# First and third norm by token halves in a two-block transformer kernel

## The chip, the cores and the metric

The kernel runs on one core of a Trainium2 chip. The metric is the device time in microseconds (us), from the first to the last instruction with what lies around them; the table below gives the median of three runs. TensorE is called PE, VectorE DVE, ScalarE ACT, GpSimd POOL and SyncE SP, as in the profile.

## What is computed

512 tokens of width 1024 pass through two transformer blocks. What matters here is the end of the first block and the start of the second:

```python
h = h + rms_norm(mix @ w_out[l], ln_attn_post[l])      # first norm
hn = rms_norm(h, ln_ffn_pre[l])                        # second norm
u = causal_dwconv(hn @ w_up[l], conv_w[l], conv_b[l])
gate, val = jnp.split(u, 2, axis=-1)
f = (jax.nn.gelu(gate, approximate=True) * val) @ w_down[l]
h = h + rms_norm(f, ln_ffn_post[l])                    # third norm
...
h = rmsnorm(x, norm_mix_g[l])                          # fourth norm, second block
proj = h @ w_in                                        # the stage "mix"
a = a_val * jax.nn.sigmoid(a_gate)
a = causal_dwconv_2(a, conv_a_w) + conv_a_b            # 31 taps
```

`rms_norm` divides by the root of the mean square over the 1024 features of a token, then scales by a gain. (The kernel numbers the input's norm 0, so the four above are r = 1, 2, 3 and 4.)

## The kernel before

Activations lie transposed: 128 features on the partitions, 512 tokens along the free dimension, so 1024 features are eight tiles `[128, 512]`. Weights stream from memory as blocks of 1 MB, each of two output tiles by up to eight input tiles, in a ring of four slots. Every product is made of three matmuls with fp32r operands (`mm3`, L478): upper part by upper part, and the two mixed products. So each weight block is split: ACT copies it to `wh` (`split_hi` L1263, the instruction is L1273), DVE subtracts that from the raw block to get `wl` (`low` L1968, L1976). `ahead(n)` (L1275) on ACT splits block n+3. SP loads a block once the block four before it has left its slot (`load` L381 waits for `acc_ready`). Each engine works through its own list in program order; the order is written out by hand, and semaphores tie the lists together. Nothing is planned at run time.

A block of 8 input tiles is 48 matmuls of 512 columns (8 inputs, 2 outputs, 3 products); the last products of a block of the feed-forward group 2 have 6 input tiles, so 36. Results go to four banks `acc`, of which ACT evacuates each (`take` L1288, instruction L1294, and `taken_out` L1543); a block that wants a bank waits for that evacuation (`begin_block` L488).

A norm after a product (r = 1 and 3) takes these steps. The squares of the last output tiles are made by ACT (L1541, L1307) and added by DVE into `sqa` (`add_squares` L1886). PE sums over features with four tiny products (`norm_sums` L525), ACT takes the root (`norm_root` L1309), DVE the reciprocal (`norm_recip` L1895), PE spreads it over all partitions (`norm_spread` L532), and DVE adds the residual (`residual` L1937: per feature tile a scaled product L1941 and an addition L1943). Between these steps PE runs products with constants whose result is not used (`keep_busy` L484, called in `norm` L540).

The norm after it (r = 2 and 4) is not waited for at first: the first two weight blocks of the next stage are multiplied with the new residual itself, scaled by the gain (`raw_blocks` L547). ACT makes the upper part `XRH` (`raw_upper` L1330), DVE the lower part `XRL` (`raw_low` L1948, L1951), ACT the squares, and PE sums them over features, one matmul of ones per feature tile, within the first block (L562). When all eight are summed, ACT takes the root (L1318), DVE the reciprocal of 128x512 (L1898), and DVE and ACT make the normed operands `XH`, `XL` (`operand` L1907, `operand_upper` L1325), which the third block on reads. The results of the two raw blocks are scaled afterwards (`by_rms` L1955).

The lists around this, in order. ACT (L1550 to L1569): for each out block the split ahead and the evacuations; the root of norm 1; eight times copy and square; `ahead` for block ffn+3; root of norm 2; evacuation of the first two tiles; eight operand copies; then the groups of the feed-forward (`group` L1571), where the gelu of pair 0 (L1589) comes before the split ahead and the evacuation of tiles 2 and 3. DVE (L2325 to L2331, L2416 to L2428): sums of squares, reciprocal, `residual`, the lower part of block ffn+2 and of ffn+3, reciprocal of norm 2, `operand`, group 0 with its convolution (`conv3` L2334). For r = 3 and 4 the lists are alike, with `mix` for `ffn`; after `operand(4)` DVE has the taps of the 31-tap convolution (L2445), the gates and the lower weight parts up to the stage's end.

Of the kernel before, what the change touches and what calls it, by code (L numbers as in the profile page):

```python
# [62 lines left out]
OTHERS = {r: sum(x not in SUMMED for x in range(r + 1)) for r in range(9)}  # L63

NARROW = {r: sum(x not in WIDE for x in range(r + 1)) for r in range(9)}

RAW = {0: 0, 2: KT, 4: 2 * KT, 7: 3 * KT}
# [35 lines left out]
def build(nc, xT, memT, wstream, params, consts, lora, poolw, normf, out):  # L103
    with ExitStack() as ctx:
# [205 lines left out]
        def raw_of(r, k):  # L310

            return (X0H[:, k, :], X0L[k // 4][:, k % 4, :]) if r == 0 else (XRH[:, k, :], XRL[:, k, :])
# [162 lines left out]
        def _(pe):  # L475
# [49 lines left out]
            def norm_sums(r, nt=TT):  # L525

                pe.wait_ge(sq_used, KT * (r + 1))
# [12 lines left out]
            def norm(r):  # L540
                keep_busy(mb[:, 3, :], 4 if r == 1 else 12)
                norm_sums(r)
                keep_busy(mb[:, 3, :], 2)
                norm_spread(r)
                keep_busy(mb[:, 3, :], 12)

            def raw_blocks(name, r):  # L547

                for b in range(2):
                    n, t = B0[name] + b, T0[name] + 2 * b  # L550
                    begin_block(n, t)
                    for k in range(KT):
# [7 lines left out]
                        if b == 0 and r in SUMMED:  # L560
                            pe.wait_ge(sq_ready, KT * r + k + 1)
                            mm(mb[:, 0, :], ones, sq[:, k % 2, :], start=(k == 0),  # L562
                               stop=(k == KT - 1)).then_inc(sq_used, 1)
                        elif b == 0 and k == KT - 1:
                            pe.wait_ge(sq_used, KT * (r + 1))
                            mm(mb[:, 0, :], ones, sqa[:, :], start=True, stop=True).then_inc(st_sum, 1)
# [338 lines left out]
            for b in range(1, 4):  # L905
# [8 lines left out]
            norm(1)  # L914


            def group(name, i, hidden, need=None, spread=None, first=0):
# [13 lines left out]
                for b in range(4):  # L931
# [291 lines left out]
            with pe.If(crowded > 0):  # L1223
# [5 lines left out]
                pe.wait_ge(x_ready, 32 + KT)  # L1229
# [12 lines left out]
        def _(act):  # L1242
# [66 lines left out]
            def norm_root(r, nt=TT, preload=True):  # L1309
# [3 lines left out]
                if r in WIDE:  # L1313
                    if r in SUMMED:
                        act.wait_ge(sq_used, KT * (r + 1))
                    else:
                        act.wait_ge(st_sum, OTHERS[r])
                    actv(sqa[:, :], mb[:, 0, :], ACT.Sqrt, bias=cs("eps", 0, 1), scale=1.0 / D).then_inc(sd_ready, 1)  # L1318
# [4 lines left out]
                actv(sd[:, 0:nt], sums, ACT.Sqrt, bias=cs("eps", 0, 1), scale=1.0 / D).then_inc(sd_ready, 1)  # L1323

# [218 lines left out]
            def taken_out(t, dst):  # L1543
                actv(dst, acc[:, t % 4, :], ACT.Copy).then_inc(evac, 1)
# [5 lines left out]
            for b in range(4):  # L1550
                ahead(B0["out"] + b)
                for m in (2 * b, 2 * b + 1):
                    squared_out(T0["out"] + m, 8 + m)
                    if b < 3:
                        taken_out(T0["out"] + m, Fo[:, m, :])
            for m in (6, 7):
                taken_out(T0["out"] + m, Fo[:, m, :])
            norm_root(1)

            for m in range(KT):  # L1560
                act.wait_ge(x_ready, m + 1)
                raw_upper(2, m, "ln_ffn_pre")
                square(16 + m, XT[:, m, :])
# [4 lines left out]
            for k in range(KT):  # L1568
                operand_upper(2, k)  # L1569

            def group(name, i, hidden):  # L1571
# [4 lines left out]
                for b in range(hidden + 4):  # L1576
# [13 lines left out]
                    if b >= hidden and k == 2 and name == "ffn":  # L1590
                        for m in (2 * (b - hidden), 2 * (b - hidden) + 1):

                            act.wait_ge(s["acc_added"], m + 1)
                            square(24 + m, Fo[:, m, :])
# [4 lines left out]
            norm_root(3)  # L1599

            for m in range(KT):
                act.wait_ge(x_ready, 8 + m + 1)
                raw_upper(4, m, "norm_mix")
                square(32 + m, XT[:, m, :])
# [61 lines left out]
            for k in range(KT):  # L1666
                square(40 + k, MT[:, k, :])
# [6 lines left out]
            for m in range(KT):  # L1674
                act.wait_ge(x_ready, 16 + m + 1)
                square(48 + m, XT[:, m, :])
# [25 lines left out]
            def x_parts(b):  # L1702
                for m in (2 * b, 2 * b + 1):
                    act.wait_ge(x_ready, 24 + m + 1)
                    actv(XRH[:, m, :], XT[:, m, :], ACT.Copy).then_inc(s["rx_hi"], 1)
                    square(56 + m, XT[:, m, :])
# [160 lines left out]
        def _(dve):  # L1867
# [27 lines left out]
            def norm_recip(r, nt=TT):  # L1895
                dve.wait_ge(sd_ready, r + 1)
# [10 lines left out]
            def operand(r, gname):  # L1907

                dve.wait_ge(rb_ready, r + 1)
# [27 lines left out]
            def residual(r, gname, gnext):  # L1937

                dve.wait_ge(rb_ready, r + 1)
                for m in range(KT):  # L1940
                    link(v.scalar_tensor_tensor(out=tmp[:, m % 2, :], in0=Fo[:, m, :], scalar=pr(gname, m),  # L1941
                                                in1=mb[:, 1, :], op0=ALU.mult, op1=ALU.mult))
                    v.tensor_tensor(XT[:, m, :], XT[:, m, :], tmp[:, m % 2, :], ALU.add).then_inc(x_ready, 1)  # L1943
                    if m:
                        raw_low(r + 1, m - 1, gnext)
                raw_low(r + 1, KT - 1, gnext)
# [378 lines left out]
            for m in range(KT):  # L2325
# [3 lines left out]
            norm_recip(1)  # L2329
            dve.wait_ge(in_xb, 32)  # L2330
            residual(1, "ln_attn_post", "ln_ffn_pre")  # L2331
# [18 lines left out]
            def group(name, i, hidden, last=False):  # L2350
# [45 lines left out]
                for m in range(KT):  # L2396
                    if last and name == "ffn" and m >= 2:
                        add_squares(24 + m - 2)
                    dve.wait_ge(evac, add(t0 + 2 * hidden + m + 1, 24))
                    e = ev[:, (e0 + 2 * hidden + m) % 4, 2:S + 2]  # L2400
                    if name == "ffn" and k == 0:
# [10 lines left out]
                if last and name == "ffn":  # L2412
# [603 lines left out]
```

## Time and profile before

| | |
|---|---|
| median of 3 runs | 1656.53 us (1651.3 to 1659.92) |
| profiled execution, its time | 1651.62 us |
| its span, first to last instruction | 1649.7 us |
| PE, DVE, ACT busy | 1528.5, 1095.7, 705.2 us |
| mean granted PE clock | 0.987 of full speed |
| traffic | 181.37 MB, mean 110 GB/s |

PE counts as busy while any matmul is in flight, the filler of `keep_busy` too; the record of a pipelined matmul overlaps the next, so the pace is read from the distance of two starts. A row "[1.10 <-DVE XRL L1951]" says that the engine stood idle for 1.10 us until that instruction released it. The page's chain of work that ended last follows the releases back from the end: what stands in it set the time.

### The profile page before, as it was taken

The numbers are of one execution on the slowest core, as the hardware profiler recorded it, in microseconds if no ns is written. First come the engines' busy times: TensorE is split into PE (matmuls) and PEld (weight loads), VectorE is DVE, ScalarE is ACT, GpSimd is POOL, SyncE is SP. The second block draws the span as 40 slices with busy tenths as digits, with TensorE's granted clock in tenths as the row PEclk, the third lists the DMA queues.
The fourth block names the chain that finished last, engine by engine and source line by source line (L and its number), as shares of the span: only waits on it lengthen the run. The fifth ranks groups of instructions, "written<-read, shape, count | busy, mean of one in ns | idle before, by whom it ended". The sixth has DMA issues, their size and how long they took to land.

```text
span 1649.7 us, 26802 instructions
## 1 busy us (share of the span) xinstructions
PE 1528.5 (93%) x11012; PEld 1283.9 (78%) x11012; DVE 1095.7 (66%) x1661; ACT 705.2 (43%) x1057; POOL 62.4 (4%) x53
## 2 busy tenths in 40 slices
PE   5999988998999999999999999999999889889892
PEld 4889776876878888888878787877799657788892
DVE  5831667686489647737689998354765436677875
ACT  5422334444354333333454232334344345367783
POOL 0000000000000000000000000000000000222221
PEclk9999999999999999999999999999999999999996
DMA  6220000002422222222312222232234202478895
GB/s 250 102 90 13 2 2 3 3 3 78 153 77 79 101 102 102 90 90 102 128 51 103 100 79 102 77 126 92 102 128 154 77 18 85 164 244 309 313 315 188
DMA packets 37831, 181.37 MB, mean 110 GB/s; under 512 B 6342, under 2 KB 6470, under 8 KB 24400
## 3 DMA queue, kind: packets, MB, share of 16 engines
q1 hardware_dynamic: 30672, 167.08, 28.6%
q0 software_dynamic: 4864, 8.40, 1.5%
q10 hardware_dynamic: 2176, 4.19, 0.7%
q8 instruction: 87, 1.43, 0.4%
q14 instruction: 32, 0.26, 0.0%
HBM read 175.46 MB, written 12.58 MB: 114 GB/s over the span
## 4 chain that ended last, share of the span: by engine, by line
PE 71%; DVE 18%; ACT 4%; DMA 4%; issue 3%; POOL 0%; DVEq 0%; POOLq 0%; SPq 0%; ACTq 0%
PE acc L480 18%; PE acc L482 18%; PE acc L481 18%; DMA raw<-wstream 3%; DVE CA L2445 2%; PE acc L731 2%; PE mb L731 1%; DVE wl L1976 1%; DVE wl L1964 1%; PE acc L1038 1%; PE mb L562 1%; ACT wh L1273 1%; ACT wh L1260 1%; PE mb L480 1%; PE mb L481 1%
## 5 line engine op out<-in xcount | busy, mean ns | idle before, releaser
L480 PE MATMUL acc<-XH,wh 128*128 128x512 f32 x1008 | 396.2, 393 | 2.3 <-DVE wl L1976 1.3
L482 PE MATMUL acc<-XH,wl 128*128 128x512 f32 x1008 | 392.3, 389 | 0.0
L481 PE MATMUL acc<-XL,wh 128*128 128x512 f32 x1008 | 392.2, 389 | 0.0
L1273 ACT ACTIVATE wh<-raw 128x2048 fp32r<-128x2048 f32 x99 | 189.4, 1915 | 241.6 <-DMA raw<-wstream 241.6
L1976 DVE TENSOR_TENSOR wl<-raw,wh 128x2048 fp32r<-128x2048 f32 x99 | 226.1, 2287 | 67.2 <-ACT wh L1273 64.0
L480 PEld LDWEIGHTS acc<-XH,wh 128*128 128x128 f32 x1008 | 189.3, 188 | 44.6 <-issue 3.3
L481 PEld LDWEIGHTS acc<-XL,wh 128*128 128x128 f32 x1008 | 189.3, 188 | 40.6 <-issue 1.9
L482 PEld LDWEIGHTS acc<-XH,wl 128*128 128x128 f32 x1008 | 189.2, 188 | 39.6
L1294 ACT ACTIVATE ev<-acc 128x512 f32<-128x512 f32 x146 | 85.6, 598 | 218.7 <-PE acc L482 189.6
L1964 DVE TENSOR_TENSOR wl<-raw,wh 128x1024 fp32r<-128x1024 f32 x96 | 116.3, 1221 | 31.7 <-ACT wh L1260 23.7
L1260 ACT ACTIVATE wh<-raw 128x1024 fp32r<-128x1024 f32 x96 | 101.0, 1061 | 20.8 <-DMA raw<-wstream 19.0
L480 PE MATMUL acc<-wh,XH 128*128 128x256 f32 x320 | 94.2, 294 | 3.2 <-DVE tmp L2777 2.6
L482 PE MATMUL acc<-wh,XL 128*128 128x256 f32 x320 | 90.4, 283 | 0.0
L481 PE MATMUL acc<-wl,XH 128*128 128x256 f32 x320 | 90.4, 282 | 0.0
L2445 DVE SCALAR_TENSOR_TENSOR CA<-APAD,par,CA 128x512 f32<-128x512 f32 x120 | 82.1, 746 | 0.5
L480 PE MATMUL acc<-HH,wh 128*128 128x512 f32 x176 | 68.5, 389 | 0.0
L481 PE MATMUL acc<-HL,wh 128*128 128x512 f32 x176 | 68.5, 389 | 0.0
L482 PE MATMUL acc<-HH,wl 128*128 128x512 f32 x176 | 68.5, 389 | 0.0
L480 PEld LDWEIGHTS acc<-wh,XH 128*128 128x128 f32 x320 | 61.1, 191 | 4.0 <-DVE wl L1964 1.8
L481 PEld LDWEIGHTS acc<-wl,XH 128*128 128x128 f32 x320 | 61.2, 191 | 0.0
L482 PEld LDWEIGHTS acc<-wh,XL 128*128 128x128 f32 x320 | 61.1, 191 | 0.0
L444 POOL MEMSET XSL<- 128x4096 f32 x1 | 3.5, 3512 | 1397.6 <-PE mb L482 1397.6
(534 smaller groups left out, 2796.8 us busy)
## 6 DMA issues: line engine op xcount, KB each, us to landing
raw<-wstream SPq DMA_DIRECT2D x99, 1024.0 KB
raw<-wstream SPq DMA_DIRECT2D x96, 512.0 KB
YG<-YT ACTq DMA_DIRECT2D x8, 512.0 KB
XT<-xT SPq DMA_DIRECT2D x2, 1024.0 KB, 9.6
XT<-xT SPq DMA_DIRECT2D x1, 2048.0 KB, 7.7
XD<-HN SPq DMA_DIRECT2D x4, 512.0 KB, 2.6
out<-XTK SPq DMA_DIRECT2D x4, 512.0 KB, 2.6
cst<-consts SPq DMA_DIRECT2D x1, 1230.0 KB, 18.4
```

The source lines that it names most:

```text
L480: mm(out_, a[0], b[0], start=start, stop=False)
L481: mm(out_, a[0], b[1], start=False, stop=False)
L482: return mm(out_, a[1], b[0], start=False, stop=stop)
L562: mm(mb[:, 0, :], ones, sq[:, k % 2, :], start=(k == 0), stop=(k == KT - 1)).then_inc(sq_used, 1)
L731: last = mm(out_[hp(c), t * HD:(t + 1) * HD], left(hp(c), t), right(hp(c), t), start=True, stop=True)
L1038: last = mm(acc[:, v, :], VX[:, j, h * 256 + v * P:h * 256 + (v + 1) * P], PTx[:, j, :], start=(j == 0), stop=(j == 1))
L1260: actv(wh[:, slot, 4 * h:4 * h + 4].rearrange("p a b c -> p (a b c)"), raw[:, slot, h * BLK // 2:(h + 1) * BLK // 2], ACT.Copy).then_inc(h ...
L1273: actv(wh[:, n % RING].rearrange("p a b c -> p (a b c)"), raw[:, n % RING, :], ACT.Copy).then_inc(hi_done, 1)
L1294: actv(ev[:, ring, 2:S + 2], acc[:, bank, :], func, scale=scale).then_inc(evac, 1)
L1964: v.tensor_tensor(wl[:, slot, 4 * h:4 * h + 4].rearrange("p a b c -> p (a b c)"), raw[:, slot, c], wh[:, slot, 4 * h:4 * h + 4].rearrange( ...
L1976: v.tensor_tensor(wl[:, slot].rearrange("p a b c -> p (a b c)"), raw[:, slot, :], wh[:, slot].rearrange("p a b c -> p (a b c)").bitcast(F3 ...
L2445: ins = v.scalar_tensor_tensor(out=CA[:, c, :], in0=x, scalar=w, in1=CA[:, c, :], op0=ALU.mult, op1=ALU.add)
```

## The change

PE multiplies the last block before norms 1 and 3 by token halves of 256 (first half for both outputs, then the second), and so the first two raw blocks behind it: half 0 for blocks 0 and 1, then half 1 for blocks 0 and 1. One bank now holds one half of both last outputs. Sums, root, reciprocal, spreading, residual, raw operands and squares are made per half; the sums of norm r for half 0 stand inside the last block, those for half 1 inside the first raw block. The filler `keep_busy` around these two norms is gone. The rows of `XRH` and `XRL` are turned round, so that an operand does not overwrite what is still read. The semaphore counts follow. ACT's square of the last two tiles of half 1 and its evacuation come after the first two copies of half 0; the preloaded square-root table stands earlier.

The diff, cut to its core:

```diff
+HALVED = (1, 3)
+def parts_of_norms(r, left_out=()):
+    return sum(2 if x in HALVED else 1 for x in range(r + 1) if x not in left_out)
...
+RESIDUAL = {1: 0, 3: 2 * KT, 5: 4 * KT, 7: 5 * KT, 8: 6 * KT}
+SQ0 = {0: 0, 1: KT, 2: 2 * KT, 3: 4 * KT, 4: 5 * KT, 5: 7 * KT, 6: 8 * KT, 7: 9 * KT}
+AHEAD = {2: (2, 6), 4: (6, 6)}
...
@@ PE
-            def norm(r):
-                keep_busy(mb[:, 3, :], 4 if r == 1 else 12)
-                norm_sums(r)
-                keep_busy(mb[:, 3, :], 2)
-                norm_spread(r)
-                keep_busy(mb[:, 3, :], 12)
+            def half_sums(r, h):
+                pe.wait_ge(sq_used, SQ0[r] + KT - 1 + h)
+                for t in (2 * h, 2 * h + 1):
+                    last = mm(mb[:, 0, t:t + 1], sqa[:, t * P:(t + 1) * P], ones[:, 0:1], start=True, stop=True)
+                last.then_inc(st_sum, 1)
+            def half_spread(r, h):
+                pe.wait_ge(rs_ready, NARROW[r] - 1 + h)
...
+            def last_block(n, t, kt, operand_of, r, sums_at, spread_at):
+                begin_block(n, t)
+                for h in range(2):
+                    for j in range(2):
+                        for k in range(kt):
+                            a, b = operand_of(k)
+                            last = mm3(acc[:, (t + h) % 4, tok_half(j)], (wh[:, n % RING, k, j, :], wl[:, n % RING, k, j, :]),
+                                       (a[:, tok_half(h)], b[:, tok_half(h)]), k == 0, k == kt - 1)
+                            if (h, j, k) == (1, *sums_at):
+                                half_sums(r, 0)
+                            if (h, j, k) == (1, *spread_at):
+                                half_spread(r, 0)
+                    last.then_inc(acc_ready, 1)
+            def raw_halves(name, r):
+                for h in range(2):
+                    for b in range(2):
+                        n, t = B0[name] + b, T0[name] + 2 * b
+                        if h == 0:
+                            begin_block(n, t)
+                        for k in range(KT):
+                            if b == 0:
+                                pe.wait_ge(s["rx_lo"], RAW[r] + KT * h + k + 1)
+                            hi, lo = raw_of(r, k)
+                            for j in range(2):
+                                last = mm3(acc[:, (t + j) % 4, tok_half(h)], ...)
+                                if h and k == KT - 1:
+                                    last.then_inc(acc_ready, 1)
+                            if b == 0:
+                                pe.wait_ge(sq_ready, SQ0[r] + KT * h + k + 1)
+                                mm(mb[:, 3, tok_half(h)], ones, sq[:, k % 2, tok_half(h)], start=(k == 0),
+                                   stop=(k == KT - 1)).then_inc(sq_used, 1)
+                            if (h, b, k) == (0, 0, 1):
+                                half_sums(r - 1, 1)
+                            elif (h, b, k) == (0, 0, 3):
+                                half_spread(r - 1, 1)
...
-            norm(1)
+            last_block(B0["out"] + 3, T0["out"] + 6, KT, lambda k: (MX[k][0], MX[k][1]), 1, (0, 5), (1, 1))
-            raw_blocks("ffn", 2)
+            raw_halves("ffn", 2)
-            group("ffn", 2, 6)
-            norm(3)
-            raw_blocks("mix", 4)
+            group("ffn", 2, 6, final=True)
+            last_block(B0["ffn"] + 33, T0["ffn"] + 66, 6, lambda k: (HH[:, k, :], HL[:, k, :]), 3, (1, 2), (1, 5))
+            raw_halves("mix", 4)
@@ ACT
-                        act.wait_ge(sq_used, KT * (r + 1))
+                        act.wait_ge(sq_used, SQ0[r] + 2 * KT)
+            def half_root(r, h):
+                act.wait_ge(st_sum, OTHERS[r] - 1 + h)
...
+            def upper_half(r, h, m, gname):
+                act.wait_ge(x_ready, RESIDUAL[r - 1] + KT * h + m + 1)
+                actv(raw_of(r, m)[0][:, tok_half(h)], XT[:, m, tok_half(h)], ACT.Copy, ...)
+            def upper_halves(r, gname, other_half):
+                def square_half(h, m):
+                    q = SQ0[r] + KT * h + m
+                    act.wait_ge(sq_used, q - 1)
+                    actv(sq[:, m % 2, tok_half(h)], XT[:, m, tok_half(h)], ACT.Square).then_inc(sq_ready, 1)
+                for m in range(2):
+                    upper_half(r, 0, m, gname)
+                other_half()
+                square_half(0, 0)
+                for m in range(2, KT):
+                    upper_half(r, 0, m, gname)
+                    square_half(0, m - 1)
+                    if m == 3:
+                        half_root(r - 1, 1)
+                square_half(0, KT - 1)
+                for m in range(KT):
+                    upper_half(r, 1, m, gname)
+                    square_half(1, m)
...
+            ahead(B0["out"] + 3)
+            actv(sml[:, 60:61], cs("eps", 0, 1), ACT.Sqrt)
+            def out_half(h):
+                squared_out(T0["out"] + 6 + h, 14 + h)
+                taken_out(T0["out"] + 6 + h, Fo[:, 6:8, tok_half(h)])
+            out_half(0)
+            half_root(1, 0)
+            upper_halves(2, "ln_ffn_pre", lambda: out_half(1))
             ahead(B0["ffn"])
             norm_root(2)
...
+                        if name == "ffn" and k == 2 and b == hidden + 3:
+                            half_squared(j)
+                            if j == 0:
+                                half_root(3, 0)
@@ DVE
+            def half_squares(q, h):
+                dve.wait_ge(sq_ready, q + 1)
+                dve.wait_ge(sq_used, q)
+                link(v.tensor_tensor(sqa[:, tok_half(h)], sqa[:, tok_half(h)], sq[:, q % 2, tok_half(0)], ALU.add))
+                v.tensor_tensor(sqa[:, tok_half(h)], sqa[:, tok_half(h)], sq[:, q % 2, tok_half(1)], ALU.add).then_inc(sq_used, 1)
...
+            def residual_halves(r, gname, gnext):
...
+                for h in range(2):
+                    dve.wait_ge(rb_ready, NTH[r] - 1 + h)
+                    for m in range(KT):
+                        link(v.scalar_tensor_tensor(out=tmp[:, m % 2, tok_half(h)], in0=Fo[:, m, tok_half(h)], ...))
+                        v.tensor_tensor(XT[:, m, tok_half(h)], XT[:, m, tok_half(h)], tmp[:, m % 2, tok_half(h)],
+                                        ALU.add).then_inc(x_ready, 1)
+                        if m:
+                            low_half_of(h, m - 1)
+                        if h == 0 and m == 1:
+                            half_squares(SQ0[r] + 7, 1)
+                        if h == 0 and m == 3:
+                            half_recip(r, 1)
+                    low_half_of(h, KT - 1)
...
-            residual(1, "ln_attn_post", "ln_ffn_pre")
+            residual_halves(1, "ln_attn_post", "ln_ffn_pre")
             lows(B0["out"] + 6)
```

## Rows read from the trace of the kernel before

**Rows 1.** Page, part 4: shares of the chain that ended last, by engine.

```profile
PE 71%; DVE 18%; ACT 4%; DMA 4%; issue 3%; POOL 0%; DVEq 0%; POOLq 0%; SPq 0%; ACTq 0%
```

**Rows 2.** Chain of waits, 400 to 1010 us: start us, us, what.

```profile
479.27 0.70 ACT sqa L1318
479.99 3.36 DVE sqa L1898
...
500.84 0.97 ACT ev L1294 x2
...
857.49 0.70 ACT sqa L1318
...
943.62 2.21 DVE wl L1976
```

**Rows 3.** Waits of PE, 490 to 1010 us: us in total, times, longest.

```profile
PE acc L480 <- ACT ev L1294: 1.8, 2, 0.9
...
PE acc L480 <- DVE wl L1976: 1.3, 1, 1.3
```

**Rows 4.** Timeline of PE, first norm: start us, us, what, [idle before <-releaser].

```profile
441.89 0.39 PE L480 MATMUL acc<-MX,wh 128*128 128x512 f32 x1
...
452.55 0.39 PE L482 MATMUL acc<-MX,wl 128*128 128x512 f32 x1
...
454.46 1.05 PE L529 MATMUL mb<-cst,sqa 128*128 128x1 f32 x8 [0.64 <-DVE sqa L1893]
...
456.08 1.16 PE L536 MATMUL mb<-cst,sml 128*128 128x128 f32 x8
...
461.02 0.47 PE L480 MATMUL acc<-XRH,wh 128*128 128x512 f32 x1 [1.10 <-DVE XRL L1951]
```

**Rows 5.** Timeline of PE, third norm.

```profile
828.46 2.84 PE L486 MATMUL mb<-cst 128*128 128x128 f32 x24
...
839.26 0.47 PE L480 MATMUL acc<-XRH,wh 128*128 128x512 f32 x1 [1.02 <-DVE XRL L1951]
```

**Rows 6.** Timeline of ACT, both norms.

```profile
448.29 1.92 ACT L1273 ACTIVATE wh<-raw 128x2048 fp32r<-128x2048 f32 x1 [4.82 <-DMA raw<-wstream]
...
475.32 1.90 ACT L1273 ACTIVATE wh<-raw 128x2048 fp32r<-128x2048 f32 x1
...
825.44 1.92 ACT L1273 ACTIVATE wh<-raw 128x2048 fp32r<-128x2048 f32 x1 [1.82 <-DMA raw<-wstream]
827.98 1.28 ACT L1294 ACTIVATE ev<-acc 128x512 f32<-128x512 f32 x2 [0.62 <-PE acc L482]
829.49 0.63 ACT L1307 ACTIVATE sq<-Fo 128x512 f32<-128x512 f32 x1 [0.24 <-DVEq L2411]
```

**Rows 7.** Timeline of DVE, first norm.

```profile
457.36 0.75 DVE L1941 SCALAR_TENSOR_TENSOR tmp<-Fo,par,mb 128x512 f32<-128x512 f32 x1 [1.33 <-PE mb L536]
...
477.25 2.29 DVE L1976 TENSOR_TENSOR wl<-raw,wh 128x2048 fp32r<-128x2048 f32 x1 [0.49 <-ACT wh L1273]
```

**Rows 8.** Timeline, 256 columns: DVE in a later norm, PE in a later block.

```profile
1194.78 0.47 DVE L2579 SCALAR_TENSOR_TENSOR tmp<-MT,par,mb 128x256 f32<-128x256 f32 x1
...
1195.61 0.42 DVE L1905 TENSOR_TENSOR ML<-tmp,MH 128x256 fp32r<-128x256 f32 x1
1195.96 0.48 DVE L2579 SCALAR_TENSOR_TENSOR tmp<-MT,par,mb 128x256 f32<-128x256 f32 x1
...
1212.44 0.28 PE L480 MATMUL acc<-MH,wh 128*128 128x256 f32 x1
...
1215.43 0.28 PE L481 MATMUL acc<-ML,wh 128*128 128x256 f32 x1
```

**Rows 9.** Stretches from a PE pause on: length, PE, PEld, DVE, ACT, POOL busy, PEclk, DMA.

```profile
1473.60:1486.00 12.40, 9.01 (x51) 8.95 (x51) 6.79 (x7) 5.22 (x7) 6.15 (x4) 0.72 0.66 234
175.60:184.00 8.40, 6.76 (x168) 6.77 (x170) 7.30 (x15) 1.19 (x4) 0.00 (x0) 0.80 0.01 2
30.00:38.40 8.40, 5.85 (x25) 4.48 (x25) 6.46 (x4) 4.55 (x6) 0.00 (x0) 1.00 0.35 125
```

More of the change, by code:

```diff
@@ new lines, in half_spread @@
+            def half_spread(r, h):
+                pe.wait_ge(rs_ready, NARROW[r] - 1 + h)
+                for t in range(2):
+                    last = mm(mb[:, 1 + h, t * P:(t + 1) * P], rs[:, 2 * h + t:2 * h + t + 1].to_broadcast([P, P]), ident,
+                              start=True, stop=True)
+                last.then_inc(rb_ready, 1)
+            def last_block(n, t, kt, operand_of, r, sums_at, spread_at):
[11 more added lines that the diff above has]
+                    last.then_inc(acc_ready, 1)
@@ L559, in raw_blocks @@
                                 last.then_inc(acc_ready, 1)
[L560 to L564, printed above, removed]
+                        if b == 0 and k == KT - 1:
                             pe.wait_ge(sq_used, KT * (r + 1))
@@ L904, in _ @@
             out_first(MIXED[3:])
-            for b in range(1, 4):
+            for b in range(1, 3):
                 n, t = B0["out"] + b, T0["out"] + 2 * b
@@ L930, in group @@
                                 need=need if b == first else None)
-                for b in range(4):
+                for b in range(3 if final else 4):
                     block_tiles(n_of(hidden + b), t0 + 2 * (hidden + b), (B0[name] + hidden + b) % RING,
@@ L1549, in _ @@
                 split_hi(n, 16 * (n // RING + 1), TILES_TO[n - RING])
-            for b in range(4):
+            for b in range(3):
                 ahead(B0["out"] + b)
@@ L1553, in _ @@
                     squared_out(T0["out"] + m, 8 + m)
[L1554 to L1563, printed above, removed]
+                    taken_out(T0["out"] + m, Fo[:, m, :])
+            ahead(B0["out"] + 3)
[6 more added lines that the diff above has]
+            upper_halves(2, "ln_ffn_pre", lambda: out_half(1))
             ahead(B0["ffn"])
@@ L1569, in _, with half_squared @@
                 operand_upper(2, k)
+            def half_squared(h):
+                act.wait_ge(s["acc_added"], 7 + h)
+                act.wait_ge(sq_used, SQ0[3] + 5 + h)
+                actv(sq[:, h, :].rearrange("p (a c) -> p a c", a=2), Fo[:, 6:8, tok_half(h)],
+                     ACT.Square).then_inc(sq_ready, 1)
             def group(name, i, hidden):
@@ L1589, in group @@
                         actv(gl[:, b % 2, :], gl[:, b % 2, :], ACT.Gelu_apprx_tanh).then_inc(s["act_done"], 1)
-                    if b >= hidden and k == 2 and name == "ffn":
+                    if b == hidden and k == 2 and name == "ffn":
+                        actv(sml[:, 60:61], cs("eps", 0, 1), ACT.Sqrt)
+                    if hidden <= b < hidden + 3 and k == 2 and name == "ffn":
                         for m in (2 * (b - hidden), 2 * (b - hidden) + 1):
                             act.wait_ge(s["acc_added"], m + 1)
-                            square(24 + m, Fo[:, m, :])
+                            square(SQ0[3] + m, Fo[:, m, :])
             group("ffn", 0, 8)
@@ L1598, in _ @@
             group("ffn", 2, 6)
[L1599 to L1604, printed above, removed]
+            upper_halves(4, "norm_mix", lambda: None)
             ahead(B0["mix"])
@@ L1666, in _ @@
             for k in range(KT):
-                square(40 + k, MT[:, k, :])
+                square(SQ0[5] + k, MT[:, k, :])
             for b in range(4):
@@ L2324, in _ @@
             low(B0["out"] + 2)
-            for m in range(KT):
+            for m in range(6):
                 add_squares(8 + m)
@@ L2411, in group @@
                         v.nop().then_inc(s["acc_added"] if name == "ffn" else x_ready, 1)
-                if last and name == "ffn":
-                    add_squares(24 + KT - 2)
-                    add_squares(24 + KT - 1)
             low(B0["ffn"] + 3)
```

92 lines of the change are left out of this document (57 added, 35 removed).

## The prediction

> **What bounds the kernel now.** I read the page first: PE is in 71% of the chain that ended last and DVE in 18% [rows 1], so the question is in which stretches the chain runs through DVE. The chain from 400 to 1010 us answers it. In each of the two places that the change touches, the chain leaves PE at the moment when the squares of the next norm (r = 2, r = 4) are summed, 479.25 and 857.45, and comes back only much later [rows 2]. Behind the second norm it goes root, reciprocal, operands, convolution, gelu, split, evacuation, and PE starts block ffn+3 when that evacuation is over, 501.8; PE had waited 0.9 for it. Behind the fourth it stays on DVE until the lower weight part of 943.62 is done at 945.8; PE had waited 1.3 for that [rows 2, 3]. Call T the end of the sum of squares. Since both chains start at T and end in a PE wait, a change of T is a change of the end, as long as PE is not later on its own account. PE has slack there: from T to ffn+3 the chain takes 22.7 us, PE's own work was 21.8.
>
> The timeline of PE shows no useful product between 452.8 and 461.02, and between 828.46 and 839.26, 8.2 and 10.8 us, filled with constants [rows 4, 5]. These are not a price by themselves; T is.
>
> **Prices of half pieces.** A matmul of 512 columns starts every 0.2268 us (47 steps from 441.89 to 452.55 [rows 4]), one of 256 every 0.1196 (25 steps [rows 8]). 276 matmuls are halved (48 + 36 in the last blocks, 96 in each raw pair): 276 x (0.2392 - 0.2268) = 3.4 us more on PE. The Trainium skill (TensorE: Matmul & The Clock Gate, Back-to-back issue gap) has N/2.4 ns plus 2.5 for a gap; by it the halving would cost 276 x 2.5 ns = 0.7 us, and the sum would be 2.7 lower. The rows decide for 3.4. A sum of squares, full width: the eight steps from 461.02 to 479.25 take 2.28 each, less six matmuls of 1.36, so 0.92; half, about 0.45. The half step of the first raw block is then 0.72 + 0.45 = 1.17. DVE has a three-instruction pattern of 256 columns that repeats after 1.18 (1194.78 to 1195.96 [rows 8]); the residual's third instruction is a bit longer, so 1.25 per half tile, above PE's 1.17. Bounds for it: 1.18, and 1.43 if nothing overlaps.
>
> **First norm.** The last block starts at 441.89. Its half 0 ends at 447.6. PE goes on with half 1 and reaches the sums of half 0, put behind its sixth input tile, at 449.8. They need ACT's square of half 0. But ACT's list has the split ahead first, and that waits for a weight load until 448.29 and ends at 450.2 [rows 6]; nothing in the change brings that load forward. Then the square, 0.63 [rows 6], and DVE's two half additions, 0.45 + 0.42 [rows 8]: 451.8. **PE stands for 2.0**, and all behind it. Sums to spreading were 1.62, spreading to residual 1.28 [rows 4, 7]; with half the products some 1.16 and 0.78. The rest of the block lies between, so spreading is at 453.7, the residual starts at 454.5 (2.9 earlier than 457.36 [rows 7]) and the block ends at 456.4. Two half tiles and a lower part later, 2.2, PE can begin the raw block: 456.7, which is 4.3 earlier than 461.02.
> There the gain ends. DVE's third tile stands behind the additions for half 1, whose square ACT makes at 457.4; PE's second step waits for that, with the late square of the first tile, 1.7 in all. DVE's fifth tile stands behind the reciprocal of half 1, which waits for PE's sums; PE's fourth step waits 0.8. First raw block, half 0: 456.7 + 8 x 1.17 + 1.0 (sums and spreading) + 2.5 = 469.5. Then comes the part that the plan of loops adds: half 0 of the **second** raw block, 48 x 0.1196 = 5.7, stands ahead of half 1 of the first, and only the latter ends the sums: 469.5 + 5.7 + 9.4 = 484.6. **T is 5.4 later.**
> One more wait. Before, ACT split block ffn+3 at 475.32, DVE made its lower part by 479.5, and that was done 0.45 before the reciprocal [rows 2, 6, 7]. ACT's last square waits for PE's sum two steps back; these are now 2.3 ahead of T, no longer 4.5. So the split runs from 482.7 to 484.6, the lower part to 486.9, and the reciprocal, next in DVE's list, starts then and not at T + 0.74: 1.5 more. Reciprocal 486.9 against 479.99: **+6.9**, all of which reaches ffn+3. PE's own end of the raw blocks, 484.6 + 5.7, is 0.3 later than before, so PE waits and gains nothing.
>
> **Third norm.** The block starts at 828.46 - 36 x 0.2268 = 820.3; half 0 ends at 824.6; 27 matmuls later, 827.8, PE is at the sums. ACT again has the split first, from 825.44 on, 1.8; then the evacuation, the square 1.51 behind it (DVE adds in between), 0.63 for it [rows 6], 0.9 for DVE's additions and 0.2 of signals: 830.5. **PE stands for 2.7.** The block ends at 832.1, spreading at 832.6; half 1 is evacuated and added by 833.9, then the residual starts, and PE's first raw step at 836.15 (before, 839.26 [rows 5]). **PE stands for 3.5**, now without filler. The two waits inside the raw block are 0.9 and 0.8 (the square of half 1 is early here): 836.15 + 9.4 + 1.0 + 1.7 = 848.2, + 5.7 + 9.4 = 863.3, T later by 5.8, and with the 1.5 of the late split **+7.3**.
>
> The renumbered counters, ACT's half copies (two instructions for one) and the square-root table moved forward cost nothing on this path: ACT is in step with PE's sums. The loads of ffn+4 and mix+4 start when the first raw block leaves its slot, 5 us later than before; they have two blocks of PE work, over 20 us, as cover, and only if that were gone would a load of some 6 us (441.9 to 448.3, [rows 4, 6]) show.
>
> **The clock.** The filler kept PE at work. The stretches from a pause on [rows 9]: a pause of 3.4 was followed by a granted clock that averaged 0.72 over 12.4 us, so 6.9 us at 1.2 GHz and 3.5 lost; one of 1.6 by 0.80 over 8.4, 1.7 lost; one of 2.55 by nothing. So per pause 0 to 3.5. The third norm has pauses of 2.7 and 3.5 close together, nearest to the 3.4, so I take 3.5 there once; for the 2.0 of the first norm I take 0.
>
> **Sum.** 6.9 + 7.3 + 3.5 = 17.7. The profiled execution would go from 1651.6 to 1669.3. It was 4.9 below the median of the runs; on the median 1656.5 it gives **1674.2**.
>
> **Rivals.**
> *The clock holds* at 2.4 GHz: 14.2, 1670.7. For it: the pause of 2.55 left no trace. Chance 0.30.
> *The clock falls at both norms*: 17.7 + 1.7 to 3.5 more, some 1677. For it: the pause of only 1.6 was enough once. Chance 0.20.
> *The waits inside are not there*, for example because ACT gets its load earlier, but T still rules: then T is 479.7 and 855.3, +0.5 and -2.2, with 1.5 each +1.3 in all: 1657.8, no change. With half of the waits it is near +8. Against it: the load's arrival stands in the rows, and the order of ACT's list in the diff. Chance 0.09.
> *Faster: PE's own list is the bound.* If DVE's chain behind T had six us of slack, the end would follow PE, which without waits would end the raw blocks at 485.5 and 861.0 where it was 490.1 and 868.2: -4.6 - 7.2 = -11.8, 1644.7. It decides from the point at which the chain from T to ffn+3 is shorter than PE's 5.7 + 10.9 = 16.6; it measures 22.7 [rows 2]. Chance 0.03.
>
> **How the numbers follow.** Forecast 0.38, clock holds 0.30, falls twice 0.20: slower by over 0.5% in all three, 0.88. (0.5%, about 8 us, is what a measurement of this kernel can tell from no change.) Same 0.09, faster 0.03. The range takes in the three slow cases with DVE's step between 1.18 and 1.43 and waits shorter by a third: 1662 to 1684.
>
> **What would show it.** Right: PE waits at the half sums of about 2.0 and 2.7 for DVE's half additions, released behind ACT's split; the full root of the second norm 5.4 later after the last block's start than before (42.7 against 37.4) and of the fourth 5.8 later; DVE's reciprocal behind a lower weight part, not behind the root; a wait of some 5 us ahead of ffn+3 and of over 5 near 945; a granted clock of half in the stretch behind the third norm. Wrong: the reciprocal right behind the root; PE without a wait at ffn+3; an end that moves with PE's gaps and not with T.

## Result and profile after

The kernel after takes **1678.37 us** (median of 4 runs, 1673.3 to 1682.58), the kernel before 1658.22 (4 runs, 1651.3 to 1660.9) beside it: ratio 1.0134, 95% interval 1.0112 to 1.0156. The forecast was slower, by 17.7; the medians differ by 20.2. That difference of the medians is known to some 4 us either way. The profiled execution took 1673.3, its span is 1671.5 (before 1651.6 and 1649.7).

The page of the kernel after, busy time and shares of the chain that ended last (before: [rows 1]):

```profile
PE 1533.6 (92%) x11232; PEld 1301.6 (78%) x11232; DVE 1103.3 (66%) x1715; ACT 710.4 (42%) x1091; POOL 60.6 (4%) x53
...
PE 68%; DVE 19%; ACT 4%; DMA 4%; issue 4%; POOL 0%; DVEq 0%; POOLq 0%; SPq 0%; ACTq 0%
```

The chain has moved from PE towards DVE. Where, the waits of PE show, 430 to 1040 us of the kernel after (us in total, times, longest):

```profile
PE acc L502 <- DVE XRL L2066: 5.2, 4, 3.5
PE acc L502 <- DVE wl L2113: 4.9, 2, 3.6
PE mb L566 <- DVE sqa L2053: 4.6, 2, 2.7
PE acc L502 <- ACT ev L1361: 4.5, 2, 3.5
PE acc L502 <- DVE XL L2033: 4.4, 2, 2.2
PE mb L611 <- ACT sq L1410: 0.8, 1, 0.8
```

The third and the sixth row are the half sums and a half square; the first is the start of the raw blocks and two waits inside the first of them. The other three stand *behind* T, 13.8 in all, where before had 1.8 and 1.3 [rows 3]. (T is, as in the prediction, the end of the sum of squares; the rows below give the start of its last matmul pair, 0.6 earlier.) In order of time, PE of the kernel after (start, us, what, [idle before <- releaser]):

```profile
442.33 0.28 PE L502 MATMUL acc<-MX,wh 128*128 128x256 f32 x1
...
452.35 0.61 PE L566 MATMUL mb<-cst,sqa 128*128 128x1 f32 x4 [1.95 <-DVE sqa L2053]
...
458.45 0.28 PE L502 MATMUL acc<-XRH,wh 128*128 128x256 f32 x1
...
470.83 0.59 PE L611 MATMUL mb<-sq,cst 128*128 128x256 f32 x2
...
477.74 0.60 PE L611 MATMUL mb<-sq,cst 128*128 128x256 f32 x2
...
485.74 0.59 PE L611 MATMUL mb<-sq,cst 128*128 128x256 f32 x2
...
494.27 0.47 PE L502 MATMUL acc<-XH,wh 128*128 128x512 f32 x1 [2.19 <-DVE XL L2033]
...
510.54 0.47 PE L502 MATMUL acc<-XH,wh 128*128 128x512 f32 x1 [3.54 <-ACT ev L1361]
...
830.49 0.28 PE L502 MATMUL acc<-HH,wh 128*128 128x256 f32 x1
...
840.87 0.61 PE L566 MATMUL mb<-cst,sqa 128*128 128x1 f32 x4 [2.67 <-DVE sqa L2053]
...
846.59 0.55 PE L502 MATMUL acc<-XRH,wh 128*128 128x256 f32 x1 [3.49 <-DVE XRL L2066]
...
873.48 0.59 PE L611 MATMUL mb<-sq,cst 128*128 128x256 f32 x2
...
964.00 0.79 PE L502 MATMUL acc<-XH,wh 128*128 128x512 f32 x1 [3.55 <-DVE wl L2113]
...
1000.40 0.47 PE L502 MATMUL acc<-CH,wh 128*128 128x512 f32 x1 [0.98 <-ACT ev L1361]
```

PE waits 1.95 for DVE's half additions and starts the raw block 16.1 behind the last block (before 19.1 [rows 4]): the change does bring the raw block forward. The last square sum of half 0 is at 470.83, the first of half 1 at 477.74. Those 6.91 are one step of 1.15 and the 48 matmuls of the second raw block's half 0, 5.76, which push the last sum (485.74) back. Behind T, DVE and ACT of the kernel after:

```profile
484.19 4.49 DVE L2113 TENSOR_TENSOR wl<-raw,wh 128x2048 fp32r<-128x2048 f32 x2
488.60 3.35 DVE L2009 RECIPROCAL sqa<-sqa 128x512 f32<-128x512 f32 x1
```
```profile
448.89 1.92 ACT L1340 ACTIVATE wh<-raw 128x2048 fp32r<-128x2048 f32 x1 [4.97 <-DMA raw<-wstream]
...
450.80 0.58 ACT L1642 ACTIVATE sq<-acc 128x512 f32<-128x512 f32 x1
...
484.41 1.90 ACT L1340 ACTIVATE wh<-raw 128x2048 fp32r<-128x2048 f32 x1
...
486.37 0.69 ACT L1385 ACTIVATE sqa<-mb,cst 128x512 f32<-128x512 f32 x1
```

The root is done at 487.06, but the reciprocal starts at 488.60, when DVE's two lower parts are through. The square of half 0 stands behind a split that waited 4.97 for its load.

For all kernels below I cut the profiled execution at four events that each trace shows: A from the last block's start to DVE's reciprocal of the second norm, B from there to the start of the third norm's last block, C from there to the reciprocal of the fourth norm, D from there to the first product with CH. Before the change these are 38.1, 340.3, 37.9 and 121.5, 537.8 in all (479.99 - 441.89, 820.30 - 479.99, 858.21 - 820.30, 979.69 - 858.21). In after, 46.3, 341.9, 45.9 and 124.1, 558.1 (488.60 - 442.33, 830.49 - 488.60, 876.34 - 830.49, 1000.40 - 876.34): **+20.3**. The two profiled spans differ by 21.8; 0.4 of the rest lies ahead of the last block and 1.1 behind the CH product. That the medians differ by 20.2 agrees, within their 4 us. A and C hold the norms. B and D have the same work in both kernels; what they gained is the clock, as the run with filled waits shows below.

Stretches of the kernel after at the lower clock (length, PE, PEld, DVE, ACT, POOL busy, PEclk, DMA share, GB/s):

```profile
454.00:457.00 3.00, 3.00 (x16) 3.00 (x15) 1.13 (x3) 0.19 (x1) 0.00 (x0) 0.50 0.00 0
495.00:498.00 3.00, 3.00 (x8) 2.35 (x8) 2.93 (x5) 1.48 (x3) 0.00 (x0) 0.50 0.45 191
512.00:515.00 3.00, 3.00 (x8) 2.32 (x7) 2.86 (x5) 0.00 (x0) 0.00 (x0) 0.50 0.00 0
847.00:849.00 2.00, 2.00 (x9) 1.77 (x9) 1.93 (x6) 0.81 (x2) 0.00 (x0) 0.50 0.00 0
963.00:969.00 6.00, 5.00 (x12) 3.94 (x13) 6.00 (x9) 1.91 (x1) 0.00 (x0) 0.50 0.28 119
```

Each belongs to one of the waits above, 1.95, 2.19, 3.54, 3.49 and 3.55: the clock fell at the end of the wait, or up to 1.6 before or behind it. The first four lasted 3.4 us each, the last one 6.8, from 962.5 to 969.3. A granted clock of 0.50 is 1.2 GHz, 1.00 is 2.4.

### The profile page after: what moved, and what is told of

It reads as the page before. It is cut to its first block, busy times and chain, and to the rows that moved or that the text cites. A ratio compares the mean times of both kernels' runs of the same rounds, so it can differ in the third digit from the quotient of the medians.

```text
span 1671.5 us, 27330 instructions
## 1 busy us (share of the span) xinstructions
PE 1533.6 (92%) x11232; PEld 1301.6 (78%) x11232; DVE 1103.3 (66%) x1715; ACT 710.4 (42%) x1091; POOL 60.6 (4%) x53
## 4 chain that ended last, share of the span: by engine, by line
PE 68%; DVE 19%; ACT 4%; DMA 4%; issue 4%; POOL 0%; DVEq 0%; POOLq 0%; SPq 0%; ACTq 0%
PE acc L502 18%; PE acc L504 18%; PE acc L503 18%; DMA raw<-wstream 3%; DVE CA L2585 2%; PE acc L798 2%; DVE wl L2101 2%; DVE wl L2113 2%; PE mb L798 1%; PE acc L1105 1%; ACT wh L1340 1%; ACT wh L1327 1%; PE mb L502 1%; PE mb L683 1%; PE mb L504 1%
## 5 line engine op out<-in xcount | busy, mean ns | idle before, releaser
L503 PEld LDWEIGHTS acc<-XL,wh 128*128 128x128 f32 x1008 | 190.7, 189 | 41.3 <-issue 2.2
L502 PE MATMUL acc<-HH,wh 128*128 128x512 f32 (+1 forms) x188 | 70.7, 376 | 0.0
L503 PE MATMUL acc<-HL,wh 128*128 128x512 f32 (+1 forms) x188 | 70.6, 375 | 0.0
L504 PE MATMUL acc<-HH,wl 128*128 128x512 f32 (+1 forms) x188 | 70.6, 375 | 0.0
```

What stands on the lines that cost most here:

```text
L502: mm(out_, a[0], b[0], start=start, stop=False)
L503: mm(out_, a[0], b[1], start=False, stop=False)
L504: return mm(out_, a[1], b[0], start=False, stop=stop)
```

## The experiments

There were ten runs, eight kernels and both originals once more, each profiled. The four cuts of all, in us of one profiled execution (where the third norm is as before the change, its last block's start is taken 36 matmuls of 0.2268 ahead of the filler behind it), and the ratio of the medians to the kernel before:

```
                      A      B      C      D     sum    ratio (95%)
before              38.10  340.31  37.91  121.48  537.80
before again        38.10  340.27  37.93  121.46  537.76
after               46.27  341.89  45.85  124.06  558.07  1.0134 (1.0112-1.0156)
after again         44.67  341.90  47.29  124.39  558.25
blocks in turn      40.07  341.91  41.18  122.87  546.03  1.0046 (1.0029-1.0064)
split behind        42.70  343.19  45.12  124.32  555.33  1.0100 (1.0069-1.0131)
lows early          43.99  342.18  46.47  123.10  555.74  1.0123 (1.0075-1.0172)
filler behind T     44.20  341.90  46.94  122.99  556.03  1.0125 (1.0091-1.0160)
filled waits        44.82  340.34  45.19  121.46  551.81  1.0080 (1.0056-1.0104)
first norm only     44.57  341.89  38.40  121.52  546.38  1.0044 (1.0026-1.0061)
turn + split        38.01  341.90  39.96  123.06  542.93  1.0027 (1.0014-1.0040)
first, turn + split 38.02  340.30  37.93  121.51  537.76  0.9996 (0.9984-1.0007)
```

**Blocks in turn: does T rule?** PE's order of two loops, nothing else:

```diff
-                for h in range(2):
-                    for b in range(2):
+                for b in range(2):
+                    for h in range(2):
```

> The kernel after, but PE finishes both halves of the first raw block before it begins the second (loop over blocks outside, over halves inside), in both norms; nothing else is changed. If T, the end of the sum of squares, sets the end: T comes 48 x 0.1196 = 5.7 earlier in each norm, less what DVE's pace (1.25 per half tile against PE's 1.17) takes back, up to 0.6; the two waits behind each T (2.2 + 3.5 in both norms) go, and with them the falls of the clock that cost 1.6 and 2.6. Against the profiled run of the kernel after, 1673.3, some -10.5 to -15.5: about 1660, near 1.005 of the kernel before. If T does not matter and PE's own list does: no change, since PE has exactly the same matmuls, 1673.

Measured 1663.92 (10 runs) beside 1656.02, ratio 1.0046; -12.0 in the cuts. PE and DVE of this kernel:

```profile
476.68 0.59 PE L611 MATMUL mb<-sq,cst 128*128 128x256 f32 x2
...
477.83 0.60 PE L611 MATMUL mb<-sq,cst 128*128 128x256 f32 x2
...
502.76 0.47 PE L502 MATMUL acc<-XH,wh 128*128 128x512 f32 x1 [1.92 <-ACT ev L1361]
```
```profile
476.39 4.49 DVE L2113 TENSOR_TENSOR wl<-raw,wh 128x2048 fp32r<-128x2048 f32 x2
480.80 3.35 DVE L2009 RECIPROCAL sqa<-sqa 128x512 f32<-128x512 f32 x1
```

PE has exactly the same matmuls, and the kernel is 12 faster (14 by the medians); some 3 of the 12 are the clock, 1.7 of the fall at 454 and 1.2 in D. T rules, and the rival that PE's own list does falls. From the raw block's start the last sum comes 22.2 later, in runs with the order of the change 27.0: 4.8 earlier, not 5.7. The missing 0.9 is DVE, whose pace (1.25 a half tile: in half 1 the sums here follow each other by 1.24 to 1.26, in after by 1.14) PE no longer has time to wait out.

**Filler behind T: has PE slack there?**

```diff
                                    stop=(k == KT - 1)).then_inc(sq_used, 1)
+                                if (h, k) == (1, KT - 1):
+                                    keep_busy(mb[:, 0, :], 24)
```

> The kernel after, with 24 multiplications of constants, 5.7 us, on PE directly behind the last sum of squares (behind T), in both norms. If T sets the end and PE has 5.7 us of slack behind it (2.2 + 3.5 of waits): the 11.4 us of added work cost nothing, the waits behind T go, and the clock no longer falls behind them, -2 to -4: 1669 to 1671. If PE's own list sets the end: +11.4, 1685.

PE of this kernel:

```profile
485.25 5.52 PE L508 MATMUL mb<-cst 128*128 128x128 f32 x48
...
509.64 0.47 PE L502 MATMUL acc<-XH,wh 128*128 128x512 f32 x1 [2.20 <-ACT ev L1363]
```

Measured 1678.37 (4 runs). That is 11 us of added work, two times 5.52, and the ratio is 1.0125 where after has 1.0134: the work cost nothing, but the gain of 2 to 4 that was expected does not show in the medians either; by the cuts it is 2 faster. From the reciprocal (487.68) to ffn+3 it takes 21.96; before, 479.99 to 501.95 is 21.96 too (its row: `501.95 0.47 PE L480 MATMUL acc<-XH,wh 128*128 128x512 f32 x1 [0.94 <-ACT ev L1294]`), blocks in turn 480.80 to 502.76 again 21.96, after 21.94. Whatever PE does in between, this stretch keeps its length: it is DVE's and ACT's chain.

**Split behind: what do the half sums wait for?** ACT's list, first norm (the third likewise):

```diff
-            ahead(B0["out"] + 3)
             actv(sml[:, 60:61], cs("eps", 0, 1), ACT.Sqrt)
...
             half_root(1, 0)
+            ahead(B0["out"] + 3)
             upper_halves(2, "ln_ffn_pre", lambda: out_half(1))
```

> The kernel after, with ACT's split of the block three ahead moved behind the evacuation, square and root of half 0 of the last block, in both norms. If that split is what PE waits for at the half sums: the waits of 2.0 and 2.7 there go (to under 0.8), T and the end come 2.0 and some 1.5 to 2.7 earlier (in the third norm a part may turn into the wait ahead of the raw block, which half 1's evacuation sets), 3.5 to 4.7 in all, 1669. If the half sums wait for something else (the evacuation itself, DVE's additions): the waits stay and the time stays at 1673, or rises by the split that now stands before the residual's first half.

Measured 1672.39 (4 runs), 1.0100. PE of this kernel:

```profile
440.94 0.28 PE L502 MATMUL acc<-MX,wh 128*128 128x256 f32 x1
...
448.86 0.50 PE L566 MATMUL mb<-cst,sqa 128*128 128x1 f32 x4
...
453.79 0.35 PE L502 MATMUL acc<-XRH,wh 128*128 128x256 f32 x1 [0.30 <-DVE XRL L2067]
```

The wait at the first half sums is gone, in the third norm it falls from 2.67 to 0.45 while the one ahead of the raw block grows from 3.49 to 4.27. The raw blocks begin 12.9 and 14.7 behind the last block; in after again it is 14.8 and 16.8 (16.1 in after). That is the -2.0, and -1.4 or more, that the split was said to cost. A longer fall of the clock in B (343.2; 6.8 us long where the others had 3.4) gave 1.3 of it back.

**Lows early: is the reciprocal 1.5 late?**

```diff
                 for m in range(KT):
+                    if m == 2:
+                        ahead(B0["ffn" if r == 2 else "mix"])
                     upper_half(r, 1, m, gname)
...
+                        if h == 1 and m in (0, 3):
+                            low(B0["ffn" if r == 1 else "mix"] + 2 + (0, 3).index(m))
```

> The kernel after, with ACT's split and DVE's lower part of block ffn+3 (mix+3), and DVE's lower part of ffn+2 (mix+2), moved from behind the last square to the start of the second half, where ACT and DVE are ahead of PE; both norms. If the reciprocal is 1.5 late because these stand before it: DVE's reciprocal starts within 0.3 of the root's end instead of 1.5 behind it, 1.5 earlier in each norm, and the waits at ffn+3 and near 964 shrink by as much: -3.0, 1670. Rival: the 4.5 us of lower parts delay the second half of the residual, PE waits there tile by tile, and T goes back by up to 2 in each norm: 1673 to 1677.

DVE and PE of this kernel:

```profile
489.28 3.35 DVE L2009 RECIPROCAL sqa<-sqa 128x512 f32<-128x512 f32 x1 [2.71 <-ACT sqa L1385]
```
```profile
487.93 0.59 PE L611 MATMUL mb<-sq,cst 128*128 128x256 f32 x2
```

Measured 1678.18 (4 runs, 1668.6 to 1683.03), above both values that were expected, though the interval of the ratio reaches down to them. Each mechanism was half right. The reciprocal now waits for the root and starts 1.35 behind T's last sum instead of 2.86, so the 1.5 is real; but the last sum is 27.75 behind the raw block's start instead of 26.99, since DVE, at its own pace in half 1, had to fit 4.5 of lower parts in. Some 0.75 per norm is left, too little for this measurement (1.0123, interval 1.0075 to 1.0172).

**Filled waits: is it idleness that lowers the clock?** Fillers ahead of the half sums and of the third norm's raw block, behind the raw pairs and ahead of ffn+3 and mix+3:

```diff
                             if (h, j, k) == (1, *sums_at):
+                                keep_busy(mb[:, 3, :], 8 if r == 1 else 11)
...
+                    if (name, i, b) == ("ffn", 0, 3):
+                        keep_busy(mb[:, 0, :], 14)
...
+            keep_busy(mb[:, 0, :], 8)
             group("ffn", 0, 8, need=(xn_ready, 9), first=2)
...
+            keep_busy(mb[:, 3, :], 14)
             raw_halves("mix", 4)
+            keep_busy(mb[:, 0, :], 8)
+            block_tiles(B0["mix"] + 2, T0["mix"] + 4, ..., need=(xn_ready, 17))
+            keep_busy(mb[:, 0, :], 14)
```

> The kernel after, with multiplications of constants laid into PE's waits: 8 and 11 (0.237 each) ahead of the half sums, 14 ahead of the third norm's raw block, 8 behind each raw pair and 14 ahead of ffn+3 and mix+3. If the idle stretches are what makes the clock fall, the falls of the profiled run of after at 454, 495, 511, 846 and 962 go; two of them cost time that is seen (1.6 and 2.6) and the one at 454 some 1.2: -4 to -6, ratio to the kernel before near 1.010. If the falls have another cause (the load on PE itself): they stay, and the time stays at 1.013. If the fillers stand in PE's way: above 1.013.

Measured 1671.0 (6 runs), the kernel before 1655.01 beside it, ratio 1.0080; its interval lies wholly below that of after. The window from 430 to 1000 us of after and of this kernel:

```profile
430.00:1000.00 570.00, 546.00 (x2636) 460.62 (x2634) 415.16 (x562) 214.27 (x278) 0.00 (x0) 0.98 0.25 89
```
```profile
430.00:1000.00 570.00, 560.53 (x2816) 475.96 (x2815) 418.91 (x570) 216.67 (x281) 0.00 (x0) 1.00 0.26 91
```

No fall is left in it, B and D are back at 340.3 and 121.5, and the time falls by 6.3 in the cuts, just above what was expected. What remains against before is A + C, 14.0: the price of the change without the clock.

**First norm only: are the two prices separate?** The third norm with its last block, fillers, residual and raw blocks as before the change, and the counters to fit:

```diff
-HALVED = (1, 3)
+HALVED = (1,)
...
-            group("ffn", 2, 6, final=True)
-            last_block(B0["ffn"] + 33, ...)
-            raw_halves("mix", 4)
+            group("ffn", 2, 6)
+            norm(3)
+            raw_blocks("mix", 4)
```

> The change in the first norm alone; the third norm, its last block, residual and raw blocks as before the change, with their fillers. By the steps of the prediction +6.9; by the reciprocals of four runs that have the change, 6.1 to 8.2, depending on whether the clock falls inside the last block: ratio 1.004 to 1.005, and from the last block's start to the reciprocal 44.2 to 46.3 where before has 38.1; in the third norm 37.9 as before. If the two norms' costs are not separate (counters, loads, buffers shared): the third norm would differ from 37.9.

Measured 1663.2 (7 runs), 1.0044; A 44.57, so +6.5, and C 38.4, 0.5 above before, with a fall of the clock in it, from 841.9 to 845.3. The two norms pay separately. That fall is also the one exception to the fillers: the third norm had all of them, its longest wait was 1.48, and the clock fell all the same. Before, before again and first, turn + split ran the same norm with the same fillers and had none.

**Turn + split, in both norms and in the first alone**: the edits of blocks in turn and of split behind together.

> Both changes that gave time, together: PE finishes both halves of the first raw block before the second, and ACT's split comes behind half 0 of the last block. If they add up: against the first of them alone (ratio 1.0046) another -2.0 and -1.5 or so, ratio 1.002 to 1.003, 1660; from block start to reciprocal 38 in the first norm and 40 in the third. If DVE's pace of 1.25 takes it back (PE then waits tile by tile): 1.0046 as before.

> The same two changes in the first norm alone, the third as before the change. By the measured pieces the first norm takes 13.0 from the last block's start to the raw block, 22.2 to T and 2.9 to the reciprocal, 38.1, what the kernel before takes: ratio 0.999 to 1.001. If the raw block begins earlier and T keeps up fully (no pacing by DVE), up to 2 less: 0.998. If the halves cost something that these pieces leave out: 1.003 or more.

Measured 1659.28 (12 runs), 1.0027, A 38.0 and C 40.0, and for the first norm alone 1655.27 (12 runs), 0.9996, A 38.0. The gains add up. PE and DVE of the first norm alone:

```profile
444.91 0.28 PE L502 MATMUL acc<-MX,wh 128*128 128x256 f32 x1
...
457.76 0.36 PE L502 MATMUL acc<-XRH,wh 128*128 128x256 f32 x1 [0.30 <-DVE XRL L2076]
...
479.95 0.60 PE L618 MATMUL mb<-sq,cst 128*128 128x256 f32 x2
```
```profile
478.53 4.49 DVE L2134 TENSOR_TENSOR wl<-raw,wh 128x2048 fp32r<-128x2048 f32 x2
482.93 3.34 DVE L2019 RECIPROCAL sqa<-sqa 128x512 f32<-128x512 f32 x1
```

The raw block begins 12.9 behind the last block where before needs 19.1, 6.3 earlier. DVE then needs 16 half tiles at 1.25, the additions and the reciprocal of half 1, 22.2 to the last sum where full tiles took 17.2, 461.02 to this row of before:

```profile
478.21 1.02 PE L562 MATMUL mb<-sq,cst 128*128 128x512 f32 x2
```

With two lower parts behind them the reciprocal comes 3.0 behind that sum instead of 1.8. 5.0 and 1.2 are what was gained ahead of the raw block: it is spent on DVE. None of these kernels beats the kernel before.

**Both kernels again**: does the clock fall in the same places each time?

> The kernel before, profiled a second time. If what PE does fixes which pauses the clock falls behind: the same stretches at 1.2 GHz as in the first profile (178 to 181, 1413 to 1416, 1478 to 1485, the end). If the same pause falls in one run and not in the next: other stretches, and a time that moves by what they cost; from 430 to 1000 still none, since its pauses there are filled and its waits 1.5 at most. 1651 to 1661 either way, and from the reciprocal to ffn+3 21.96 again.

> The kernel after, profiled a second time. From the last block's start to the reciprocal 44.2 to 44.6 in the first norm if the clock holds in the last block (four kernels with the same list had that), 46.3 if it falls there again; the third norm 45.2 to 47; reciprocal to ffn+3 21.95. Falls of the clock between 430 and 1000 again, in at least three places, not all the same. 1673 to 1683.

1655.58 and 1676.96 (one run each). Before again had A to D as before to 0.04, but no fall at 178, and late in the program falls at 1342, 1403, 1417 and 1478 us instead of 1413 and 1478, and 676.1 from the CH product to the end of the span instead of 670.0. After again had none at 454 (A 44.67) and none at 495, but 10 us at 839 to 849 (C 47.29) and again the ones behind ffn+3 and mix+3. So which pause is followed by a fall differs from run to run; the fall in the first norm's last block came once and not again.

## Why the prediction was right, and where it was off

- *T is 5.4 later, and all of it reaches ffn+3*: right in kind, a little high in size. Blocks in turn, the filler and the constant 21.96 show that T and DVE's chain set the end, with PE's list far off it. From block start to the last sum 43.4 in the profiled run, 41.3 to 42.0 in those with the same order and no fall in the last block; the prediction had 42.7 to the *end* of the sum, which is 0.6 behind its start, so 44.0 in the profiled run and 41.9 to 42.6 in the others. Before has 37.4: T is 4.6 to 5.2 later with the clock held, 6.6 with the fall.
- *PE stands for 2.0 and 2.7 behind ACT's split, 3.5 ahead of the third raw block*: 1.95, 2.67 and 3.49 (after again 1.73, 2.77 and 3.08). The split is the cause of the first two, as moving it shows. Inside the first raw block PE stood for 0.76, 0.68 and 0.53, 2.0 in all, where the prediction had 1.7 and 0.8, 2.5.
- *The second raw block's half 0, 48 x 0.1196 = 5.7, stands ahead of T*: 5.76. By the rule of the Trainium skill (TensorE: Matmul & The Clock Gate, Back-to-back issue gap), N/2.4 ns plus 2.5, which the page gives for an isolated matmul, an estimate is 5.2. The trace does not agree, and decides for the row, as the prediction did. The prediction's "2.7 lower" by that rule does not follow from its own sum: the 3.4 us are no term of it, and 48 of the 276 halved matmuls, half 1 of the second raw blocks, stand behind T.
- *The reciprocal 1.5 late*: right in size, 1.5 behind the root's end (488.60 against 487.06), 2.86 behind the start of the last sum, and 1.35 once the split and the lower parts were moved. The prediction named only ffn+3's lower part; DVE in fact makes two in a row, 4.49.
- *First norm +6.9, third +7.3*: 6.5 (after again and first norm only, 44.6 and 44.7 against 38.1) and 7.3 (filled waits, 45.2 against 37.9; one execution).
- *Waits of some 5 ahead of ffn+3 and over 5 near 945*: 5.00 ahead of ffn+3 in after again, 3.54 in the profiled run of after, where the fall at 495 slowed PE ahead of it; the long wait in the second stage is 3.55 at 964, behind ones of 2.19 and 1.36. The prediction did not have the waits of 2.19 ahead of the third blocks.
- **The clock, +3.5, is the term that was mis-sized.** Its step took "the third norm has pauses of 2.7 and 3.5 close together" and let nothing stand for the rest. Measured: 1.7 in the first last block, 1.6 behind ffn+3 (B), 0.7 in the third norm, 2.6 behind mix+3 (D), 6.5 in after (558.07 - 537.80 - 6.5 - 7.3); after again 0.1, 1.6, 2.1, 2.9. The step failed by pricing only the pauses *ahead* of the raw blocks. The waits at ffn+3 and near 945, which the same text forecast at some 5 each, are pauses too: where no filler stood in them, every profiled kernel with both norms halved had a fall behind each. They are also the ones whose fall costs in full, since PE's work follows directly: half of the 3.4 us behind ffn+3 is 1.7, and 5.3 of the 6.8 near 963 lie behind the wait, half of which is 2.6.
- The rival that the clock holds gave 14.2; with the waits filled it is 14.0. The sum missed by 2.6 of 20.3: 3.0 more clock, 0.4 less in the first norm. That it came as near is in part luck: the 3.5 was placed in the third norm, where the clock cost 0.7 (2.1 in after again), and the waits that it left out cost 4.2.

Open: why the part behind 1000 us differs by up to 8 between kernels with the same code there (670.0 to 678.6, and 670.0 and 676.1 for the kernel before alone). The falls there move, and part of the difference goes with them: between the CH product and the last fall, which reaches to the end of the span, the clock was low for 10.2 us in before (670.0), 13.7 in after (671.1), and 17 to 31 in the other ten executions (673.0 to 678.6). Among these ten the length does not order the times, and no run was made to settle it.

## What to carry to other kernels

When work is halved so that a consumer can start early, look at the order in which the halves are then nested: here half 0 of the next block stood ahead of the half that a reduction still needed, and that alone cost some 4.5 of the 6.5 in the first norm and some 4 of the 7.3 in the third (A and C of blocks in turn against after again and filled waits). Ask next which engine the halves slow down: DVE took 1.25 for a half tile where PE took 1.15, so even with the better order the start won ahead was lost behind. And price every wait of a few us that a later end creates, not only those in the edited lines, with the clock that PE loses behind it.

## What the hardware showed

- At ffn+3, a wait of PE of 1.9 went with a fall to 1.2 GHz in two kernels (blocks in turn, turn + split: B 341.9) and not in two others with the same wait (filled waits, first with turn + split: 1.89 and 1.92, B 340.3). A wait of 5.0 went with one each time (after again, split behind, lows early, first norm only). Shorter waits are no safeguard: at 227 to 229 us, with a wait of 0.73, the clock fell in three executions (lows early, filler behind T, first with turn + split) and held in nine with the same wait.
- A fall costs by what follows it. Behind ffn+3, 3.4 us at 1.2 GHz cost 1.6. Ten us of it across the end of the third norm's last block and the start of its raw block (after again, 839.0 to 849.2) cost 2.1 (C 47.29 against 45.19 with the waits filled), not 5: a wait of 3.08 for DVE lay inside it in any case, and a wait of 0.57 inside the raw block, which filled waits has, was gone.
- DVE's and ACT's chain of 21.96 from the reciprocal to ffn+3 came out between 21.93 and 21.96 in all twelve executions, whatever the clock of PE; in after it fell inside the stretch, at 495, in lows early at 508.
